# Low parts of the projection weights on VectorE, and a last stage pipelined over tiles

## The reference

```python
mod = silu(c) @ w_ada + b_ada                     # 1024 x 6144
sh1, sc1, ga1, sh2, sc2, ga2 = split(mod, 6)
h = rmsnorm(x, ln_mix_g) * (1.0 + sc1) + sh1
(rq, rk, rv, rg, nq_, nkc, nvc, nks, nvs, nkw, nvw, ngate) = split(h @ w_in)
y_ret = retention(rope(rq), rope(rk), rv) * silu(rg)
y_nsa = nsa(nq_, nkc, ...)                        # compressed, selected, sliding
mix = concatenate([y_ret, y_nsa]) @ w_out
x = x + ga1 * mix
h2 = rmsnorm(x, ln_ffn_g) * (1.0 + sc2) + sh2
x = x + ga2 * ((silu(h2 @ w_ff_gate) * (h2 @ w_ff_up)) @ w_ff_down)
return rmsnorm(x, ln_final_g)
```

## Time and profile before

| | before |
|---|---|
| median of 3 runs | 726.59 us (726.28 to 727.12) |
| the profiled execution, its own time | 729.54 us |
| its span, first to last instruction | 727.7 us |
| mean granted TensorE clock | 0.976 of full |
| TensorE matmuls busy | 682.1 us, 94% of the span |
| VectorE / ScalarE / GpSimd busy | 332.8 / 225.5 / 265.9 us |
| HBM traffic | 85.41 MB read, 2.10 MB written |

### The profile page before, as it was taken

One profiled execution on the slowest core, in us unless ns is written; L12 is line 12 of the kernel. 1 busy time (PEld: TensorE's weight loads), 2 busy tenths in 40 slices (PEclk: granted clock), 3 DMA queues, 4 the chain that ended last, 5 costly groups with the idle time before them and its releaser, 6 DMA issues.

```text
span 727.7 us, 9019 instructions
## 1 busy us (share of the span) xinstructions
PE 682.1 (94%) x3547; PEld 564.1 (78%) x3547; DVE 332.8 (46%) x587; ACT 225.5 (31%) x378; POOL 265.9 (37%) x127
## 2 busy tenths in 40 slices
PE   2678899999989898999999999999999999999995
PEld 1556679987768687888898888888888888888884
DVE  4878999977465668152620110000000029633126
ACT  4435233422132333332542222222222213232222
POOL 2316443432000111138034434434434427545531
PEclk9699999999998899999999999999999999999999
DMA  9975986665000000176014233233233223232002
GB/s 314 359 257 152 353 293 234 199 240 228 30 2 1 0 2 1 40 221 202 1 48 127 87 96 107 87 98 104 87 102 101 89 86 117 86 103 72 0 1 116
DMA packets 73962, 88.09 MB, mean 121 GB/s; under 512 B 3048, under 2 KB 57536, under 8 KB 73792
## 3 DMA queue, kind: packets, MB, share of 16 engines
q1 hardware_dynamic: 73184, 86.36, 36.0%
q0 software_dynamic: 416, 1.08, 0.4%
q10 hardware_dynamic: 320, 0.07, 0.0%
HBM read 85.41 MB, written 2.10 MB: 120 GB/s over the span
## 4 chain that ended last, share of the span: by engine, by line
PE 78%; DVE 10%; ACT 3%; issue 3%; DMA 3%; SPq 2%; POOL 0%; POOLq 0%; DVEq 0%
PE ps L1523 11%; PE ps L1524 11%; PE ps L1522 11%; PE ps L1141 11%; PE ps L1143 11%; PE ps L1142 11%; PE ps L1274 3%; DMA raw<-in_w_in 3%; DVE acc L732 2%; DVE ps L875 1%; SPq L344 1%; PE ps L1332 1%; PE ps L1399 1%; PE ps L1228 1%; ACT hf L488 1%
## 5 line engine op out<-in xcount | busy, mean ns | idle before, releaser
L404 POOL TENSOR_TENSOR wl<-raw,wh 128x1024 fp32r<-128x1024 f32 (+1 forms) x94 | 238.6, 2543 | 285.8 <-ACT wh L456 285.6
L456 ACT ACTIVATE wh<-raw 128x1024 fp32r<-128x1024 f32 (+1 forms) x94 | 97.4, 1039 | 154.4 <-PE ps L1524 73.9
L1522 PE MATMUL ps<-hTh,wh 128*128 128x512 f32 (+1 forms) x384 | 142.8, 372 | 0.0
L1523 PE MATMUL ps<-hTl,wh 128*128 128x512 f32 (+1 forms) x384 | 142.6, 371 | 0.0
L1524 PE MATMUL ps<-hTh,wl 128*128 128x512 f32 (+1 forms) x384 | 142.6, 371 | 0.0
L1106 DVE TENSOR_TENSOR act<-ps,sg 128x512 f32<-128x512 f32 x22 | 15.2, 692 | 212.3 <-PE ps L1524 212.3
L1141 PE MATMUL ps<-wh,hTh 128*128 128x512 f32 (+1 forms) x224 | 90.5, 404 | 11.8 <-DVE hTl L770 10.6
L1143 PE MATMUL ps<-wh,hTl 128*128 128x512 f32 (+1 forms) x224 | 85.8, 383 | 0.0
L1142 PE MATMUL ps<-wl,hTh 128*128 128x512 f32 (+1 forms) x224 | 85.7, 383 | 0.0
L1522 PEld LDWEIGHTS ps<-hTh,wh 128*128 128x128 f32 x384 | 72.4, 188 | 12.5
L1523 PEld LDWEIGHTS ps<-hTl,wh 128*128 128x128 f32 x384 | 72.4, 188 | 12.4
(11 more groups left out here) (197 smaller groups left out, 818.4 us busy)
## 6 DMA issues: line engine op xcount, KB each, us to landing
raw<-in_w_ada SPq DMA_DIRECT2D x32, 512.0 KB, 5.8
raw<-in_w_ff_gate SPq DMA_DIRECT2D x22, 512.0 KB, 3.8
raw<-in_w_ff_up SPq DMA_DIRECT2D x22, 512.0 KB, 3.7
raw<-in_w_ff_down SPq DMA_DIRECT2D x22, 512.0 KB, 3.2
raw<-in_w_in SPq DMA_DIRECT2D x20, 512.0 KB, 7.0
early<-in_w_ada SPq DMA_DIRECT2D x16, 512.0 KB, 9.6
raw<-in_w_out SPq DMA_DIRECT2D x8, 512.0 KB, 6.6
xs<-in_x SPq DMA_DIRECT2D x4, 512.0 KB, 5.3
```

The lines of the kernel that those rows point to most:

```text
L404: pool.tensor_tensor(lo, raw[:, slot, 0:n], hi.bitcast(F32), ALU.subtract).then_inc(w_lo, 1)
L456: a.activation(split(u, n)[0], raw[:, slot, 0:n], ACT.Copy).then_inc(w_hi, 1)
L1522: mm(o, hi[:, ks], hTh[:, k, c0:c1], start=k == 0, stop=False)
L1523: mm(o, hi[:, ks], hTl[:, k, c0:c1], start=False, stop=False)
```

## The change

The low parts of the 24 projection units move from GpSimd to VectorE. `low(0)` to `low(3)` stand after the quarters of `ada_early`; `low(v + 3)` stands at the end of VectorE's iteration v, ahead of the `ada` pieces. GpSimd keeps the low parts from the output weights on, with a semaphore of its own (`w_lo2`); its memsets and its one bias transfer now stand ahead of them. In the last stage VectorE takes the next tile's first half before it finishes the tile before; each half is scaled into `xb` early; ScalarE scales the second half by `rstd` and sends it out itself; the last half of the last tile is cut into two pieces of 256 columns.

```diff
 # gpsimd
-            for u in range(UNITS):
+            pool.wait_ge(ada_used, ADA_OPS)
+            pool.memset(V[:, :, :, :, DH:DE], 1.0).then_inc(v_ones, 1)
+            pool.wait_ge(mlp1, 1)
+            pool.dma_start(ga2[:, :], b_ada[5 * D:6 * D].partition_broadcast(P)).then_inc(bias2_in, 16)
+            pool.wait_ge(mod_read, 8)
+            pool.memset(mcol[:, :, :], 0.0).then_inc(mcol_set, 1)
+            for u in range(U0_OUT, UNITS):
 # vector: the helper, and its three places
+            def low(u):
+                n = size(u)
+                hi, lo = split(u, n)
+                d.wait_ge(w_hi, u + 1)
+                d.tensor_tensor(lo, raw[:, place[("w", u)][0], 0:n], hi.bitcast(F32), ALU.subtract).then_inc(w_lo, 1)
             ada_early(0, range(16))
+            low(0)
             ada_early(1, range(AHEAD))
...
                     ada_early(q + 1, range(AHEAD + 5, 16))
+                    low(q + 1)
...
+                if v and v + 3 < U_IN:
+                    low(v + 3)
                 for j in ada_after.get(v + 3, []):
                     ada(j)
 # scalar, last stage
+            def finish(t):
+                a.wait_ge(y_scaled, piece_count(t, len(PIECES[t]) - 1))
+                a.wait_ge(rstd_ok, N_X2 + t)
+                a.activation(xb[:, t % 2, HALF:D], xb[:, t % 2, HALF:D], ACT.Copy, scale=rstd[:, t:t + 1]).then_inc(y_high, 1)
+                a.wait_ge(y_high, t + 1)
+                a.dma_start(out[t * P:(t + 1) * P, HALF:D], xb[:, t % 2, HALF:D]).then_inc(out_done[t], 16)
 # vector, last stage
+            def scale_final(t, n):
+                c0, c1 = PIECES[t][n]
+                if t >= 2 and n == 0:
+                    d.wait_ge(out_done[t - 2], 32)
+                d.wait_ge(x2_ok, piece_count(t, n))
+                d.tensor_tensor(xb[:, t % 2, c0:c1], x1[:, t, c0:c1], gfin[:, c0:c1], ALU.mult).then_inc(y_scaled, 1)
...
             for t in range(TT):
+                last = len(PIECES[t]) - 1
+                take(t, 0)
+                scale_final(t, 0)
+                if t:
+                    finish(t - 1)
+                then(variance_final(t, 0))
+                for n in range(1, last + 1):
+                    take(t, n)
+                for n in range(1, last + 1):
+                    if n == last and last > 1:
+                        then(variance_final(t, 1))
+                    scale_final(t, n)
+                variance_final(t, last).then_inc(var_ok, 1)
+            finish(TT - 1)
```

More of the change, by code:

```diff
@@ L207, in block_kernel @@
         ssq = small("ssq", [P, TT])
-        ssq2 = small("ssq2", [P, TT])
+        part = small("part", [P, 3])
         rstd = small("rstd", [P, TT])
@@ L312, in split, with wait_low @@
             return wh[:, u % SPLIT, 0:n], wl[:, u % SPLIT, 0:n]
+        def wait_low(engine, u):
+            if u < U0_OUT:
+                engine.wait_ge(w_lo, u + 1)
+            else:
+                engine.wait_ge(w_lo2, u - U0_OUT + 1)
         def size(u):
@@ L403, in low @@
                 hi, lo = split(u, n)
-                pool.tensor_tensor(lo, raw[:, slot, 0:n], hi.bitcast(F32), ALU.subtract).then_inc(w_lo, 1)
+                pool.tensor_tensor(lo, raw[:, slot, 0:n], hi.bitcast(F32), ALU.subtract).then_inc(w_lo2, 1)
             def power(n, buf):
@@ L682, in _ @@
                 high(U0_DOWN + f)
-            for t in range(TT):
[L684 to L690, removed]
+            def finish(t):
[4 more added lines that the diff above has]
+                a.dma_start(out[t * P:(t + 1) * P, HALF:D], xb[:, t % 2, HALF:D]).then_inc(out_done[t], 16)
+            for t in range(TT):
+                for n, (c0, c1) in enumerate(PIECES[t]):
+                    a.wait_ge(x2_ok, piece_count(t, n))
+                    if t and n == 0:
+                        a.wait_ge(var_ok, N_X2 + t - 1)
+                    a.activation(sqj[:, c0 % HALF:c0 % HALF + c1 - c0], x1[:, t, c0:c1], ACT.Square, accum_out=part[:, n:n + 1]).then_inc(sq3, 1)
+                    if t and n == 0:
+                        finish(t - 1)
+            finish(TT - 1)
         @block.vector
@@ L1117, in _, with take @@
             d.wait_ge(gfin_in, 16)
-            for t in range(TT):
[L1119 to L1124, removed]
-                d.tensor_scalar(rstd[:, t:t + 1], ssq[:, t:t + 1], 1.0 / D, EPS, ALU.mult, ALU.add).then_inc(var_ok, 1)
-                d.tensor_tensor(x1[:, t, 0:512], x1[:, t, 0:512], gfin[:, 0:512], ALU.mult).then_inc(y_scaled, 1)
-                d.wait_ge(y_scaled, t + 1)
-                d.wait_ge(rstd_ok, N_X2 + t)
-                d.tensor_scalar(xb[:, t % 2, 0:512], x1[:, t, 0:512], rstd[:, t:t + 1], None, ALU.mult)
-                d.scalar_tensor_tensor(xb[:, t % 2, 512:D], x1[:, t, 512:D], rstd[:, t:t + 1], gfin[:, 512:D],
-                                       ALU.mult, ALU.mult).then_inc(y_ok, 1)
+            def take(t, n):
+                c0, c1 = PIECES[t][n]
+                d.wait_ge(y_ps, 2 * t + c0 // HALF + 1)
+                d.tensor_tensor(x1[:, t, c0:c1], ps[:, 2 * t + c0 // HALF, c0 % HALF:c0 % HALF + c1 - c0], x1[:, t, c0:c1],
+                                ALU.add).then_inc(x2_ok, 1)
@@ new lines, in scale_final, with variance_final @@
+            def scale_final(t, n):
+                c0, c1 = PIECES[t][n]
+                if t >= 2 and n == 0:
+                    d.wait_ge(out_done[t - 2], 32)
+                d.wait_ge(x2_ok, piece_count(t, n))
+                d.tensor_tensor(xb[:, t % 2, c0:c1], x1[:, t, c0:c1], gfin[:, c0:c1], ALU.mult).then_inc(y_scaled, 1)
+            def variance_final(t, n):
+                d.wait_ge(sq3, piece_count(t, n))
+                v = rstd[:, t:t + 1]
+                if n == 0:
+                    return d.tensor_scalar(v, part[:, 0:1], 1.0 / D, EPS, ALU.mult, ALU.add)
+                return d.scalar_tensor_tensor(v, part[:, n:n + 1], 1.0 / D, v, ALU.mult, ALU.add)
```

42 lines of the change are left out of this document (21 added, 21 removed).

## The result

The changed kernel takes 719.75 us (median of 4 runs, 719.15 to 721.13); the kernel before took 726.86 beside it (4 runs, 726.28 to 729.86). The ratio is 0.9897, with a 95% interval of 0.9866 to 0.9927: 7.1 us less, where 7.2 was forecast, and 719.75 against the predicted 719.4. The interval allows a gain of 5.3 to 9.7 us, so the agreement to 0.1 us is closer than these runs can show.

The account below looks back on a forecast made before the run. TensorE was taken as the bound, busy 682.1 of 727.7 us, leaving 45.6 us without matmuls. Start 2.8, gap 2.3 and tail 2.1 sum to 7.2 us: 726.59 - 7.2 = 719.4 us, range 716.8 to 723.4.

Parts of the forecast that it names:

- What GpSimd does to VectorE: Start and projection loop: VectorE's two-input operations stand still during GpSimd's low parts, up to 2.4 us for each one met.
- the first rival: Projection: stretches aren't GpSimd's doing, VectorE becomes the bound, 738 us; decides if relief per low part is below 1.22; chance 0.06.
- Term 1, the start: Four quarters before unit 4: VectorE's operations no longer stretched, though it makes four low parts; 2.8 us less, bounds 1.0 to 4.0.
- Term 2, the gap at 87: Projection loop: TensorE's wait for the pairs goes, as shorter `ada` pieces free slots sooner; 2.3 us less, bounds 0 and 2.5.
- No cost on VectorE's path: VectorE behind 60 us: moved low parts add 17.6 us, vanished stretches take 20.1 away; nothing on the path.
- The cover of 9 us: Projection loop: VectorE gives `low(7)` at 72 and `low(8)` at 76, TensorE wants them at 81 and 87.
- Term 3, the tail: Behind the last matmul: power 1.65 us earlier, ScalarE's and VectorE's halves side by side 0.5 more; 2.1 us less, bounds 1.0 and 2.8.
- Order instead of load: Projection loop: VectorE stands at `low(6)` to `low(8)` for a transfer, the gap at 87 stays, 721.7 us; chance 0.15.
- The start gives 1: Start: the low parts lie on each quarter's chain, so only 1 us is won, 721.2 us; chance 0.12.
- the tail nothing: Last stage: waits for output halves hold VectorE up, or two smaller transfers land later, 721.5 us; chance 0.09.

Follow-up runs that it names:

- the pair of idle kernels: The changed kernel with GpSimd doing work nothing waits for: subtractions that read SBUF, 730.19 us, or memsets that only write, 720.74 us.
- the kernel with the later low parts: The changed kernel with low(1) to low(3) moved just ahead of the next quarter's first low part of h: 718.02 us, again 717.86 us.
- the last stage alone: The kernel before with only the last stage pipelined, GpSimd making all low parts: 725.93 us, ratio 0.9965.
- the start alone: The changed kernel, new last stage included, but VectorE makes only the low parts of units 0 to 3, GpSimd all others: 723.59 us.
- The experiment with two of each: The changed kernel with VectorE making every projection low part twice, only the second signalled: 732.33 us, ratio 1.0062 to the kernel before.
- the kernels with the parts apart: Parts of the change against the kernel before: projection only 722.28 us, last stage only 725.93, last stage and start 723.59, last stage and loop 721.88.
- idle writes: The changed kernel with GpSimd also running memsets that write SBUF without reading, nothing waiting for them: 720.74 us, ratio 0.9898 to the kernel before.
- idle reads: The changed kernel with GpSimd also running subtractions that read SBUF twice, nothing waiting for them: 730.19 us, ratio 1.0019 to the kernel before.
- the projection alone: The changed kernel with the last stage put back as before, only the projection's low parts moved: 722.28 us, ratio 0.9919.
- the loop alone: The changed kernel, new last stage included, but GpSimd makes the low parts of units 0 to 3, VectorE those of 4 to 23: 721.88 us.
- the power's run: The changed kernel with each tile's last variance ahead of its last multiplication by the norm's weight on VectorE: 720.04 us, a single run.

## Why the prediction was right

**What GpSimd does to VectorE: right, and shown.** The three long operations are short, no `acc<-raw` piece takes over 1.29 us, and the pair of idle kernels names the cause. The prediction sized the relief at 20.1 us from two groups "without the other groups". These two gave 15.7 and 4.3, as worked out. Another 7.3 us were in four groups that had no term: the rotated heads of 512 columns (6.6 us before, 5.5 after) and of the window keys (3.2, 1.2), half rotations of 64 columns (3.1, 0.9), and one modulation operation (2.2, 0.2). Together that is 27.3 us over 17 moved low parts, 1.6 us of relief for 1.1 of cost each: clear of the point at which the first rival decides.

**Term 1, the start: right chain, 1.9 us in this trace for 2.8.** Over the six traces with the changed order at the start it is 1.7 to 2.5. Quarter 1's modulation columns came at 44.54 where 44.5 was worked out, though quarter 0's second low part of h stands at 28.60 and not at 28.14. `low(2)` at 42.09 stands in front of them with its full 1.22, as put, and the kernel with the later low parts takes 1.1 us less for this quarter. `low(3)` was hidden, as put: behind it VectorE still waits 0.88 us. What came out shorter is the shift of quarter 2: 0.85 us at its modulation columns (54.31 for 55.16) instead of 1.75. VectorE's last piece for that sum ends at 52.29 (49.43 + 2.86), but TensorE comes to the sum only at 53.27, as it worked at half clock (0.50 from 50 to 53 us). TensorE's timeline there, after and before:

```profile
49.57 0.50 PE L1200 MATMUL ps<-wh,hTh 128*128 128x512 f32 x1 [1.30 <-DVE hTl L796]
49.91 0.57 PE L1201 MATMUL ps<-wl,hTh 128*128 128x512 f32 x1
50.28 0.63 PE L1202 MATMUL ps<-wh,hTl 128*128 128x512 f32 x1
```

```profile
51.30 0.50 PE L1141 MATMUL ps<-wh,hTh 128*128 128x512 f32 x1 [1.30 <-DVE hTl L770]
51.63 0.40 PE L1142 MATMUL ps<-wl,hTh 128*128 128x512 f32 x1
```

The waits are equally long, and the matmuls behind them 0.43 and 0.23 us apart. The prediction took TensorE's part of the chain at the clock that the trace of before has there. Quarter 3's relief of 1.05 us came as put (h's low part at 56.28 for 58.18, a shift of 1.90), so unit 3's second group came at 58.40 and not 57.5.

**Term 2, the gap at 87: gone as forecast, but the account named the wrong unit; 3.1 us for 2.3.** The prediction puts the gap down to the high part of unit 8, which it reads at 85.19. In ScalarE's code `pairs_copy(v - 5)` stands behind `high(v + 3)`, and the pairs at 87.09 are those of v = 6: they stand behind unit 9's high part, and 85.19 is unit 9's. Unit 8's came at 76.22 before and at 71.14 after; 71.4 was worked out for it, but the gap doesn't hang on it. For unit 9, the issue of its transfer before and after, and ScalarE and TensorE after:

```profile
76.14 4.87 SPq L332 DMA_DIRECT2D raw<-in_w_in  x1
```

```profile
69.04 4.98 SPq L345 DMA_DIRECT2D raw<-in_w_in  x1
79.13 1.06 ACT L466 ACTIVATE wh<-raw 128x1024 fp32r<-128x1024 f32 x1 [6.28 <-DMA raw<-in_w_in]
80.22 0.77 ACT L540 ACTIVATE pairsT<-ps 64x256 f32<-64x256 f32 x2
82.48 0.60 PE L1249 MATMUL ps<-cst,twice 128*128 128x128 f32 x4
```

The mechanism is the one that was predicted: with short pieces the slots come free sooner, the transfer is issued 7.1 us earlier and lands 6.1 us earlier. But the copy of the pairs ends at 80.99 and TensorE takes them at 82.48. That is 1.5 us of cover, not the ten that the prediction saw between 71.4 and 81, so that the whole gap went was in part luck. The loop gave 3.1 us against the kernel before, since smaller waits elsewhere in it went as well; against the kernels with the last stage alone and with the start alone it is 4.5 and 5.2, with TensorE's half clock behind their gaps in it. The sum of terms 1 and 2 at `rg` is 5.0 us in the trace, and 5.1 was predicted; the parts missed by 0.9 and 0.8 in opposite directions, and that they cancel is luck.

**No cost on VectorE's path: right, the cover was over-stated.** The cover of 9 us is that of a low part; the pairs have 1.5. The experiment with two of each shows that TensorE waits for `rg` and the rotated heads most, and 0.3 us for pairs, when VectorE has some 19 us more to do in that stretch.

**Term 3, the tail: 2.6 for 2.1.** The power started 1.6 us nearer to the last matmul than before (1.88 behind its end, 3.52 before), as predicted (1.65). Not foreseen was that it would also be shorter by 0.38, as nothing with two inputs runs beside it. The halves ran side by side; ScalarE's took 0.72 instead of 0.63, and the transfers of 256 KB 2.0 and 2.5 instead of 2.6. The wait for the output halves of two tiles before held VectorE's scaling up by 0.1 us at most, in tiles 2 and 3.

**The range.** The band of 718.0 to 720.8 that the prediction calls halves of the bounds doesn't follow from them: half-way to the three terms' bounds is 718.3 to 722.0. Nothing in the forecast rests on it.

**The rivals.** VectorE as the bound: fell, 322.0 us busy instead of 332.8. The Trainium skill (Perfetto Trace Analysis, "Optimizing Scalar/DVE Operations") says that work of a full VectorE may go to GpSimd, and that their shared port may undo the gain; for work of this kind the second half held. Order instead of load: fell, no gap at 87, though by a cover of 1.5 us. The start gives 1, the tail nothing: fell by the kernels with the parts apart. Open: why attention took 175.3 to 175.4 us in some executions (before, the last stage alone, idle writes), 174.7 with the start alone, 173.6 with idle reads, and 173.0 to 173.2 in others (the changed kernel twice, the projection alone, the loop alone, the power's run, low later twice). The granted clock from 180 to 320 us is 0.95 in the first three, 0.96 with the start alone and 0.98 in the rest. The kernel with idle writes has the changed order and still took the longer time; what lowered the clock wasn't tried.

## What to carry over

Before work is moved to GpSimd to relieve VectorE, look at the lengths of VectorE's two-input operations while GpSimd is busy: here a low part of 1024 columns took GpSimd 2.4 us or more, a low part kept VectorE from working for about 1.6 on the mean of the loop, and takes VectorE 1.2 itself. When an operation is put on an in-order engine, put it where that engine waits anyway, behind what others wait for: three low parts moved by a few instructions made the kernel 1.7 us faster, of which 1.1 are the one that stood on the chain. And when an engine's work is moved, its new cover is that of everything queued behind it, not of the moved work alone.

## What the hardware showed that I had not expected

- The exclusion between VectorE and GpSimd costs tiny operations as well: a GpSimd operation on 128x1 took 0.54 us alone, 0.66 beside a VectorE operation of 256 columns, and 0.92 beside one of 512.
- A wait's length doesn't tell TensorE's clock behind it. Behind waits of 1.28 to 1.30 us the matmuls came 0.43 us apart in some places (changed kernel at 49.57, its second trace at 49.16) and 0.23 apart in others (its second trace at 39.05, the kernel before at 51.30); behind the gap at the pairs the clock was 1.00 with 2.04 us, and 0.79 with 1.85 or 2.50. The attention stage, with the same code in every kernel, took 173.0 to 175.4 us, which is as much as a term of this prediction.
- The record of the granted clock isn't whole: from 28 to 33 us of the changed kernel it says 1.00, while the matmuls there are 0.43 us apart, as they are at a granted 0.50 from 50 to 53 us. The distance of the matmuls is the safer sign.
- Two output transfers of 256 KB, issued by SyncE and ScalarE some 0.3 us apart, landed in 2.0 and 2.5 us, where one of 512 KB took 2.6.
